# First pass' depthwise convolution on TensorE in 4 token phases by 32 channels, with a new order of projections

## The reference

```
a, gate = split(z)                    # 512 channels each
y = a * sigmoid(gate)                 # GLU
y = causal_depthwise_conv(y, w) + b   # 31 taps, one weight per tap and channel
y = layernorm(y); return silu(y)
```

## Time and profile before

| | us |
|---|---|
| median of 3 runs | 2424.86 (2422.16 to 2784.3) |
| the profiled execution, its own time | 2421.6 |
| its span, slowest core (core 2) | 2420.6 |
| spans of the 8 cores | 2413.2 to 2420.6, granted clock 0.990 to 0.992 |
| PE / DVE / ACT / POOL busy | 2333.2 / 1517.7 / 860.7 / 533.6 |

### The profile page before, as it was taken

One profiled execution on the slowest core, in us unless ns is written; L12 is line 12 of the kernel. 1 busy time (PEld: TensorE's weight loads), 2 busy tenths in 40 slices (PEclk: granted clock), 3 DMA queues, 4 the chain that ended last, 5 costly groups with the idle time before them and its releaser, 6 DMA issues.

```text
span 2420.6 us, 35366 instructions; the slowest of 8 cores (2413.2 to 2420.6 us)
## 1 busy us (share of the span) xinstructions
PE 2333.2 (96%) x11802; PEld 1099.7 (45%) x12034; DVE 1517.7 (63%) x2505; ACT 860.7 (36%) x1758; POOL 533.6 (22%) x583
## 2 busy tenths in 40 slices
PE   6998999999999999999999999999999799999998
PEld 2444444444444444444444444444444344444445
DVE  5287444899758543699939644489975764342224
ACT  3165444311135444412105545431114454331112
POOL 0050336000014235300012233600021333320000
PEclk9999999999999999999999999999999899999999
DMA  7122358443662337743464345843337324563433
GB/s 167 34 52 53 60 116 180 88 82 59 124 123 53 66 53 149 163 84 70 76 146 84 53 72 103 188 91 70 70 66 138 73 51 79 99 141 57 78 61 94
DMA packets 51218, 221.96 MB, mean 92 GB/s; under 512 B 4960, under 2 KB 9312, under 8 KB 40416
## 3 DMA queue, kind: packets, MB, share of 16 engines
q0 software_dynamic: 26640, 163.59, 38.7%
q1 hardware_dynamic: 24400, 56.10, 7.3%
HBM read 366.47 MB, written 16.78 MB: 158 GB/s over the span
## 4 chain that ended last, share of the span: by engine, by line
PE 88%; DVE 5%; DMA 3%; issue 3%; ACT 1%; SPq 0%; POOL 0%; DVEq 0%; ACTq 0%; POOLq 0%
PE psum L789 87%; DVE arena L842 2%; DVE arena L859 1%; PE psum L793 1%; DMA y<-arena 1%; DVE arena L865 1%; ACT arena L825 1%; DMA arena<-x 1%; DMA arena<-rope 1%; DVE arena L852 1%; DVE arena L1059 0%; DMA arena<-win 0%; SPq L877 0%; ACT L1534 0%; POOL arena L842 0%
## 5 line engine op out<-in xcount | busy, mean ns | idle before, releaser
L789 PE MATMUL psum<-arena 128*128 128x512 bf16 (+4 forms) x11306 | 2314.3, 364 | 77.4 <-DVE arena L842 22.6
L789 PEld LDWEIGHTS psum<-arena 128*128 128x128 bf16 (+1 forms) x11538 | 1070.9, 98 | 1307.3 <-issue 123.4
L859 DVE SCALAR_TENSOR_TENSOR arena<-arena 128x1024 f32<-128x1024 bf16 (+4 forms) x664 | 628.1, 987 | 36.3 <-ACT arena L825 24.5
L825 ACT ACTIVATE arena<-psum 128x512 f32<-128x512 f32 (+1 forms) x536 | 318.6, 598 | 923.3 <-PE psum L789 920.4
L842 POOL TENSOR_TENSOR arena<-arena 128x512 f32<-128x512 f32 (+2 forms) x328 | 407.3, 1249 | 464.7 <-DVE arena L859 364.4
L859 DVE SCALAR_TENSOR_TENSOR arena<-arena,psum 128x512 f32<-128x512 f32 (+1 forms) x288 | 196.4, 687 | 366.5 <-PE psum L789 331.2
L825 ACT ACTIVATE arena<-arena 128x512 bf16<-128x512 f32 (+6 forms) x386 | 208.8, 577 | 337.8 <-DVE arena L842 145.5
L842 DVE TENSOR_TENSOR arena<-psum,arena 128x512 bf16<-128x512 f32 (+1 forms) x288 | 194.0, 687 | 155.0 <-PE psum L789 142.9
L842 DVE TENSOR_TENSOR arena<-arena 128x4 f32<-128x4 f32 (+6 forms) x274 | 114.1, 435 | 96.2 <-ACT arena L825 90.1
L842 DVE TENSOR_TENSOR arena<-arena,psum 128x512 f32<-128x512 f32 (+2 forms) x100 | 66.1, 663 | 147.7 <-PE psum L789 145.9
L825 ACT ACTIVATE arena<-psum,arena 128x192 bf16<-128x192 f32 (+5 forms) x286 | 122.2, 439 | 80.6 <-PE psum L789 57.1
(11 more groups left out here) (21 smaller groups left out, 227.4 us busy)
## 6 DMA issues: line engine op xcount, KB each, us to landing
arena<-wgu POOLq DMA_DIRECT2D x44, 1024.0 KB, 8.8
arena<-win POOLq DMA_DIRECT2D x48, 768.0 KB, 7.9
arena<-win POOLq DMA_DIRECT2D x27, 1024.0 KB, 10.4
arena<-wdn POOLq DMA_DIRECT2D x32, 704.0 KB, 7.3
arena<-x SPq DMA_DIRECT2D x24, 512.0 KB, 9.9
arena<-wbr POOLq DMA_DIRECT2D x16, 768.0 KB, 10.2
arena<-wout POOLq DMA_DIRECT2D x8, 1024.0 KB, 13.4
xmid<-arena SPq DMA_DIRECT2D x16, 512.0 KB, 9.1
```

The costliest lines, as they stand in the source:

```text
L789: return ((lambda: nc.tensor.matmul(o.ap, lhsT=l.ap, rhs=r.ap, start=start, stop=stop)), [l, r], [o])
L825: return nc.scalar.activation(out=o.ap, in_=i.ap, func=func, **kw)
L859: vec("dve", o, nel(a), lambda: nc.vector.scalar_tensor_tensor(out=o.ap, in0=a.ap, scalar=(sc.ap if isinstance(sc, Ref) else sc), in1=b.ap ...
```

## The change

1. **Convolution of pass 0.** `glu_unit` writes its product not as tokens in a row, but into `YP` by token phase (token modulo 4). When both blocks of a chunk are done, 16 transfers on SP's queue, each of 32 partitions by 528 bytes, gather it into `YS`: for each of 16 groups of 32 channels, partition 32 p + i holds phase p of channel i. `conv_pe(c)` then runs, for each of 4 groups, 9 matmuls of 256 columns (offsets of 4 tokens), whose 128x128 weight holds the taps between 4 input and 4 output phases; `taps_unit` builds these 36 weights per chunk from a host table `convp`, in two buffers `MD`. ACT writes the result to `OS`, and 16 more transfers per chunk (32 partitions by 512 bytes) bring it back to channels on partitions, in phase order (`yCp`). `cln_unit` works on that and ACT's last step puts the tokens in order. In all 64 transfers in and 64 out.
2. **Order.** A pass' projections are one list: sc_unit chunk 0, k and v, then u and q units in turn, gv units with more sc units between, mix units, the last sc units. In pass 0 it starts with glu of chunks 0 and 1, sc_unit chunk 0, glu of chunks 2 and 3, then the convolutions with sc_unit chunk 1 between; the weights of `sc0` are loaded ahead of those of `cf1`. Attention starts with the merge (6 us before by its due time) and no more among the projections. `T["merge"]` comes 36 us earlier in pass 0 and 3 us earlier in the others.
3. **Rotary tables** of passes 1 to 3 lie in `R1 + 8192` (part of `gT`, later `yAt`), no more in `xcur`.
4. **Attention.** The probabilities of a pair are laid out so that three transposes per pair of rows do, not four (6 in place of 8 for each unit, but 4 as before for the first block); two shifted copies of V (`VP`) feed the matmuls, whose number stays.
5. **Smaller things.** `norm1_unit`'s sums of squares (H > 0) on DVE, not POOL; `cln_unit` (H > 0) during the pass before; `load_x`, `merge_last`, `wout_unit` by token block; `norm2_unit` with an earlier priority, and the second block of the first `up_unit`s later in pass 3; `final_unit` of pass 2 in four parts, 14 us apart; `convp` (320 KB) loaded at the start.

```
+    ROPE = [[fixed([HT], F32, o + i * 4096) for i in range(2)] for o in (xcur.off, R1 + 8192)]
+    VP = [fixed([9, 128], BF16, mergedT.off + 12288 + r * 2304) for r in range(2)]
+    MD = [fixed([36, 128], BF16, R1 + 24576 + i * 9216) for i in range(2)]
+    YS = fixed([16, 264], BF16, R1)
+    OS = [fixed([4, 256], BF16, R1 + 8448 + i * 2048) for i in range(2)]
+    yCp = fixed([4, HT], BF16, xcur.off + 8192)
+    YP = fixed([4, 4, 264], BF16, XS0)
...
+        dma("sp", convp.all(), convp_d, [], [convp.all()], "cp", 128 * CP_N * 4)
...
-            add = Adder(stat, 8, NB, "pool" if H else None)
+            add = Adder(stat, 8, NB, "dve" if H else None)
...
         def att_b(t):
-            todo = [(g, kb) for g in range(4) for kb in range(1 if lone else 0, 2)]
+            todo = [(pr, s) for s in range(1 if lone else 0, 3) for pr in range(2)]
...
         def glu_unit(c, b):
...
-            stt(yglu[:, c, 30 + b * NB:30 + (b + 1) * NB], sg.all(), 1.0, pa.all(), ALU.add, ALU.mult)
+            if H:
+                stt(yglu[:, c, 30 + b * NB:30 + (b + 1) * NB], sg.all(), 1.0, pa.all(), ALU.add, ALU.mult)
+                return
+            ph = lambda a: a.rearrange("p (m a) -> p m a", a=4)
+            o = YP[:, c, :, 8 + b * 128:8 + (b + 1) * 128].re(lambda a: a.rearrange("p a m -> p m a"))
+            stt(o, sg.all().re(ph), 1.0, pa.all().re(ph), ALU.add, ALU.mult)
+            if b == 1:
+                for g in range(4):
+                    for p in range(4):
+                        dma("sp", YS[32 * p:32 * p + 32, c * 4 + g, :], YP[32 * g:32 * g + 32, c, p, :], [YP[:, c, p, :]],
+                            [Mark("ys", (c * 4 + g) * 4 + p, (c * 4 + g) * 4 + p + 1)], "ys%d" % (c * 4 + g), 32 * 528, occ=0.45)
...
-        def conv_pe(c, b):
-            p = bank()
-            for k0 in range(0, 31, 8):
-                ks = range(k0, min(k0 + 8, 31))
-                pe([mmp(p.all(), dg[:, k, :], yglu[:, c, b * NB + k:b * NB + k + NB], k == 0, k == 30) for k in ks], [512] * len(ks))
+        def taps_unit(c):
+            hot = convp[:, 592:624].re(lambda a: a.rearrange("p (o t) -> p o t", o=1).to_broadcast([128, 144, 32]))
+            cw = convp[:, c * 144:(c + 1) * 144].re(lambda a: a.rearrange("p (k o) -> p k o", o=1).to_broadcast([128, 144, 32]))
+            o = MD[c % 2].all().re(lambda a: a.rearrange("p k (q t) -> p (k q) t", t=32))
+            vec("dve", o, 4608, lambda: nc.vector.tensor_tensor(out=o.ap, in0=hot.ap, in1=cw.ap, op=ALU.mult), [hot, cw])
+        def conv_pe(c):
+            for h2 in range(2):
+                p = bank((2, 256))
+                parts = []
+                for i in range(2):
+                    n = c * 4 + h2 * 2 + i
+                    for dd in range(9):
+                        fn, rd, wr = mmp(p[:, i, :], MD[c % 2][:, (h2 * 2 + i) * 9 + dd, :], YS[:, n, dd:dd + 256], dd == 0, dd == 8)
+                        parts.append((fn, rd + ([Mark("ys", n * 4, n * 4 + 4)] if dd == 0 else []), wr))
+                pe(parts, [256] * 18)
...
+                    act(OS[c % 2][:, g, :], p[:, i, :], AF.Identity, bias=convp[:, 576 + n:577 + n], scale=0.5)
+                    for q in range(4):
+                        dma("sp", yCp[32 * g:32 * g + 32, c, q * 256:(q + 1) * 256], OS[c % 2][32 * q:32 * q + 32, g, :], [OS[c % 2][:, g, :]],
+                            [Mark("yc", n * 4 + q, n * 4 + q + 1)], "yc%d" % n, 32 * 512, occ=0.45)
...
-        def final_unit(c0, n):
+        def final_unit(c0, n, js=range(8)):
...
+        if H == 0:
             unit(-60.3, lambda: wl_parts("cf0", *win(2), [xs[:, 4:6, :]]))
-            unit(-60.1, lambda: wl("cf1", *win(3), after=[xs0[:, 2:4, :]]))
+            unit(-60.1, lambda: wl("sc0", *win(6), after=[xs0[:, 2:4, :]]))
             for g in range(2):
                 for b in range(2):
                     for c in (2 * g, 2 * g + 1):
...
+                        put(3.45, lambda c=c, b=b: glu_unit(c, b))
+                if g == 0:
+                    put_w("cf1", 3)
+                    put_w("sc1", 7)
+                    put(0, ropes)
+                    put_sc(0)
+            put(0, save_hist)
+            put(4.3, lambda: conv_pe(0))
+            put(5.15, lambda: sc_unit(1, 0))
+            put(0, lambda: taps_unit(2))
+            put(4.3, lambda: conv_pe(1))
+            put(5.15, lambda: sc_unit(1, 1))
+            put(0, lambda: taps_unit(3))
+            put(4.3, lambda: conv_pe(2))
+            put(4.3, lambda: conv_pe(3))
+            put(0, fills)
+            put(0, fill_values)
+        else:
+            put_w("sc0", 6)
+            put_sc(0)
+        put(0, hist)
+        put_w("kv", 5)
+        put_w("u", 1)
+        for b in range(2):
+            put(2.0, lambda b=b: k_unit(b))
+            if b == 0:
+                put_w("q", 4)
+            put(2.4, lambda b=b: v_unit(b))
+        for i in range(8):
+            put(1.73, lambda i=i: u_unit(i // 2, i % 2))
+            put(1.95, lambda i=i: q_unit(i % 4, i // 4))
...
+        for b in range(2):
+            for ti in range(4 * b, 4 * b + 4):
+                put(1.73, lambda ti=ti: gv_unit(ti))
+            if H:
+                put(5.15, lambda b=b: sc_unit(1, b))
+            else:
+                put(1.8, lambda b=b: cln_unit(b))
+            put_w("sc%d" % (2 + b), 8 + b)
+        for c in range(2, 4):
+            for g in range(2 * c - 4, 2 * c - 2):
+                for b in range(2):
+                    put(0.3, lambda g=g, b=b: mix_unit(g, b))
+            put_sc(c)
...
-        a0, a1 = q0 + 24, T["merge"]
+        a0 = T["merge"] - 6
         step = (T["last"] - 20 - a0) / 16.0
...
-        T["merge"] = at + (100 if H else 180)
+        T["merge"] = at + (97 if H else 144)
```

More of the change, by code:

```diff
@@ L763, in build_program @@
     cstage = fixed([C_N], F32, yC.off)
+    convp = fixed([CP_N], F32, yC.off + 4096)
     p_w = pool(8192, 4, "w", True)
@@ L1036, in hist @@
             cp("pool", V[:, 0, :], V[:, 8, :])
+            for r in range(2):
+                rows = slice(r * 64, r * 64 + 64)
+                cp("dve", VP[r][rows, 0, :], V[rows, 0, :])
         ka = KA[(H + 1) % 2]
@@ L1102, in v_unit @@
             acopy(V[:, 1 + b * 4:5 + b * 4, :], p.all())
+            for r in range(2):
+                rows = slice(r * 64, r * 64 + 64)
+                acopy(VP[r][rows, 1 + b * 4:5 + b * 4, :], p[rows, :, :])
         att = {}
@@ L1262, in cln_unit @@
+        def save_hist():
+            if H:
+                cp("dve", yhist.all(), yglu[:, :, HT:HT + 30])
+                return
+            for r in range(4):
+                a, p = divmod(2 + r, 4)
+                n = 8 if r < 2 else 7
+                cp("dve", yhist[:, :, r:30].re(lambda x: x[:, :, ::4]), YP[:, :, p, 256 + a:256 + a + n])
         def cln_unit(b):
             cs = slice(b * NB, (b + 1) * NB)
+            src = yC if H else yCp
             b1, b2 = bank(), bank()
-            pe([mmp(b1.all(), onesb.all(), yC[:, c, cs], c == 0, c == 3) for c in range(4)], [512] * 4)
+            parts = [mmp(b1.all(), onesb.all(), src[:, c, cs], c == 0, c == 3) for c in range(4)]
+            if H == 0:
+                parts = [(fn, rd + [Mark("yc", c * 16, c * 16 + 16)], wr) for c, (fn, rd, wr) in enumerate(parts)]
+            pe(parts, [512] * 4)
@@ L1266, in cln_unit @@
             add = Adder(b2, 4, NB, "pool")
             for c in range(4):
-                add.square(yC[:, c, cs])
+                add.square(src[:, c, cs], [] if H else [Mark("yc", c * 16, c * 16 + 16)])
             mean = f32t()
@@ L1399, in half @@
+        at_ = T["qkv"]
+        for us, fn, lead in seq:
+            unit(at_ + lead, fn)
+            at_ += us
+        if H:
+            unit(T["qkv"] - 24, fills)
+            unit(T["qkv"] - 0.5, fill_values)
+            unit(T["qkv"] - 0.4, ropes)
+        assert abs(at_ - T["merge"]) < 3, (H, at_ - T["merge"])
+        a0 = T["merge"] - 6
         step = (T["last"] - 20 - a0) / 16.0
@@ L1462, in half @@
                 for b in range(2):
-                    unit(f0 + g * 13.8 + i * 6.9 + b * 3.45, lambda f=2 * g + i, b=b: up_unit(f, b))
+                    late = 7.0 if b and g == 0 and H + 1 == nhalf else 0.0
+                    unit(f0 + g * 13.8 + i * 6.9 + b * 3.45 + late, lambda f=2 * g + i, b=b: up_unit(f, b))
         d0 = T["down"]
@@ L1493, in half @@
             for b in range(2):
-                unit(T["qkv"] + 10 + 4 * b, lambda b=b: cln_unit(b))
+                unit(T["qkv"] - 26 + 6 * b, lambda b=b: cln_unit(b))
         for b in range(2):
@@ L1548, in _run @@
         m = {"x": np.ascontiguousarray(x[b].T)}
-        for k in ("win", "wbr", "wout", "wgu", "wdn", "small", "sgw", "sgb", "consts", "rope"):
+        for k in ("win", "wbr", "wout", "wgu", "wdn", "small", "sgw", "sgb", "consts", "rope", "convp"):
             m[k] = lay[k]
```

208 lines of the change are left out of this document (101 added, 107 removed).

## The result

The changed kernel takes 2367.31 us (median of 4 runs), the one before 2424.36 (4 runs). The ratio is 0.9764, 95% interval 0.9745 to 0.9783: 57 us or 2.4% faster. Forecast were 2361 us and -63.8. The profiled execution took 2367.09 us, its span is 2366.1 (core 4). In the new file L808 is every matmul, L812 every transpose, L844 every activation, L850 every copy on ACT, L861 tensor_tensor, L878 scalar_tensor_tensor, L896 every DMA.

What follows compares the result with a forecast made beforehand. PE was taken as the bound, with three or four stalls; -37.8 - 7 - 11 - 15 - 4 - 3 + 9 + 5 = -63.8 us gave 2357.8 against the profiled execution, 2361 for the median, range 2335 to 2398.

Steps and rivals of the forecast that it cites:

- PE as the bound, the pace of a matmul: Whole kernel: PE busy 2333.2 of 2420.6 us; matmuls take 0.2159 us with 512 columns, 0.1091 with 256.
- The way back has over 30 us ..., so nothing: Pass 0, transfers back after the convolution: over 30 us of other units precede `cln_unit`, so no wait, 0 us.
- Count no wait: Pass 0, transfers in before `conv_pe`: landing taken as 2.0 us, no wait; at 10.3 `conv_pe(3)` would wait some 3 us.
- Rival (c): Pass 0: small transfers run one after another and PE waits; slower than before from 1.4 us each; chance 0.05.
- signs of being wrong: PE waiting before `conv_pe(2)` or `conv_pe(3)`, landings of 10 us or more, k units waiting for `rope`, steady ACT waits in merge.
- Even at twice that ... it is off PE's path: Pass 0, DVE's strided GLU write: even at twice 0.69 us, 8 x 0.7, it costs PE nothing.
- Start of pass 0, +9: Start of pass 0: PE idles since convolutions no longer cover the second block's normalisation; +9 us, bounds +3 and +14.
- Middle of pass 0, -11: Middle of pass 0: q units alternating with u units and attention moved out save 11 us; bounds -4 and -15.
- Pass 3 -15, passes 1 and 2 -4, norm2 -3: Pass starts and last norm2: stalls go, -15 (bounds -8, -19), -4 (0, -8) and -3 us (0, -5).
- Transposes, -7: Attention: 60 of 64 units lose two of eight transposes; 6.7 to 9.9 us less, lower end -7 taken.
- Tables late by 2 or 3 us: Start of pass 3: the rotary table is late for the first k unit by 2 or 3 us.
- +5 for stalls I don't see: Whole kernel: allowance for unseen stalls made by the new order, +5 us, bounds 0 and +20.

Runs made afterwards that it cites:

- experiment 1: Changed kernel with DVE's GLU product in pass 0 written phase by phase (strided reads, writes in a row) instead of token by token: 2366.15 us, ratio 0.9773.
- Experiments 2: Changed kernel with half as many layout transfers, each twice as large (64 in place of 128, two chunks together): 2345.4 us, ratio 0.9687.
- experiment 3: Changed kernel with both the GLU written phase by phase and 64 layout transfers in place of 128: 2338.8 us, ratio 0.9660.
- experiment 10: Version with phase by phase GLU and 64 transfers, plus the first sc unit's weights loaded once x's first block is in: 2352.6 us, ratio 0.9712.
- (5): Changed kernel with its new order but the old convolution in pass 0 (diagonal weights, 248 matmuls, no layout transfers): 2371.6 us, ratio 0.9782.
- (6): Kernel before, only with the rotary tables of passes 1 to 3 moved out of the residual's tile: 2413.6 us, ratio 0.9961.
- (7): Kernel before, only with the attention's new layout (6 transposes in place of 8 for 60 of 64 units, shifted V copies): 2409.9 us, ratio 0.9945.
- experiment 9's second kernel: Changed kernel's new order with the old convolution, run again beside the changed kernel on the same chip: 2372.4 us, ratio 0.9795.

## Why the prediction was right, point by point

The time was within the range and 6 us from the forecast, but not by its own steps: two of them failed and two were too small, and they cancelled. That the number came out so near is luck.

- **PE as the bound, the pace of a matmul: right.** Two of the new convolution's evictions, 18 matmuls of 256 columns apart, stand at 95.78 and 97.75 us on ACT: 1.97 / 18 = 0.109 us each, as in the earlier trace rows. PE's busy time fell by 48.2 us, of which this makes 37.8 and the transposes 6.7.
- **"The way back has over 30 us ..., so nothing": this step failed.** "Count no wait", said of the transfers in, held in the changed kernel, but only since PE came late: it waits 2.48 us for one in experiment 1. The landing was about right (16.5 KB in 2.9 us, 16 KB in 1.8, medians). The 2.0 us of the Trainium skill, which the prediction sets beside its row, stand in the section that it names ("DMA: Bandwidth & Descriptors", anatomy of one DMA) for a transfer from POOL's queue, and these are from SP's. The issue was taken at 0.48 us from the rope loads and is 0.63, and above all the queue was counted by parts, 16 transfers at a time. All 128 stand in one queue from 58 to 146 us, so the first result's transfers wait behind 32 that go in. They then hold a two-deep buffer, and ACT's order carries the wait to units that have nothing to do with it. That gave waits of 9.15 and 5.26 us, and a granted clock of 0.83 and 0.90 in the stretches around and behind them. Rival (c) had the mechanism, with 1.4 us each as its point; at 0.63 it didn't make the kernel slower, but with the GLU's waits it took most of the gain. Experiments 2 and 3 show it: together they give 28 us back. None of the prediction's signs of being wrong caught it, since they look for PE waiting on the transfers themselves, and the waits reached PE through ACT.
- **"Even at twice that ... it is off PE's path": failed.** The write took 2.38 us, 3.4 times the usual 0.69, and five waits of 0.98 and one of 0.74 followed. In the changed kernel this cost nothing net, since the transfers would have held PE up anyway (experiment 1); without those it costs 6.6 us (3). The Trainium skill ("SBUF — State Buffer", the section on the DMA port swizzle) says that consecutive accesses to one 16-byte line run at full bandwidth, and that each which goes to a new line pays. The trace agrees: with a step of 528 bytes, 4.6 ns per element against 1.3, and with reads 16 bytes apart and writes in a row 1.07 us for 512, so they too pay, but less. The page gives no price for it; that the step would cost more than double, only the trace shows.
- **Start of pass 0, +9: about right.** Idle time of 3.64 and 5.85 us where before there was 2.73, at a clock of 0.93. The weights landed after 10.04 us, not 7.9. An earlier load didn't buy any of it back, but cost 14 us (10).
- **Middle of pass 0, -11: right for the order alone.** With the old convolution the 13.3 us become 2.7 (5). What the order does in it and what the smaller things do was not taken apart. In the changed kernel the transfers and one wait of 5.95 us behind the layernorm put 21.8 us back.
- **Pass 3 -15, passes 1 and 2 -4, norm2 -3: the right places, too small.** All of that idle time is gone: behind 207 us PE waited 32.8 us before (65.8 in all, less 20.0 up to 32.36 and 13.0 from there on) and 2.0 in the changed kernel (57.5 less 18.3 up to 34.3 without the wait there, and 37.2 from it to the one of 0.22 at 207.2). The reason for pass 3 was half right: the stores of y were one cause, DVE-led units the other (6).
- **Transposes, -7:** six take 0.34 us, eight 0.45, so 6.7 by the trace; alone the edit measured 11, of which 4 are open (7).
- **"Tables late by 2 or 3 us", "+5 for stalls I don't see":** no wait for the tables; the unseen stalls were the two failed steps.

The sum as measured: new order, transposes, tables and smaller things -49.6 (experiment 9's second kernel against the kernel before beside it, 2422.0), the new convolution -6.0. Of the first, tables alone are 7.5 (6) and transposes alone 11 (7); the other 31 were not taken apart further. Forecast for the first, with the start and the +5, was -26, for the second -37.8.

## What to carry to other kernels

Before work is moved from a busy engine to transfers, lay all of a stretch's issues in one line on their queue, at their price each (here 0.63 us), and look up who stands behind the last one: halving the count at the same bytes was worth 21 us, a second queue 4. A gain on the bounding engine shows only when the next limit isn't a microsecond behind, so an edit that gives nothing (the phase by phase write) should be tried again once that limit is gone. Undo one half of a change beside the whole: a sum that comes out right can hide terms that are off by over 20 us in either direction.

## What the runs showed that I had not expected

- SP issued a transfer of 32 partitions within SBUF in 0.63 us (0.67 on average) when it moved 16 KB and in 0.70 to 0.75 when it moved 33, against 0.48 for a rope load of 512 KB.
- The same scalar_tensor_tensor of 512 columns took 0.69 us with all in a row, 1.07 with reads 16 bytes apart, 2.38 with writes 528 bytes apart.
- Beside POOL's, DVE's tensor_tensors with both inputs in SBUF took 1.25 us each, where 0.69 is usual: in experiment 3 five of them took 3.16 us at 159.98, with POOL idle, and four took 4.99 here:

```profile
170.83 4.99 DVE L861 TENSOR_TENSOR arena<-arena 128x512 f32<-128x512 f32 x4 [1.44 <-ACT arena L844]
171.19 2.27 POOL L861 TENSOR_TENSOR arena<-arena 128x512 bf16<-128x512 f32 x2
```

- Loads of weights issued beside a block of x made it land in 24.5 in place of 8.3 us (experiment 10).
